# One meeting of the engines per stage boundary instead of two, with semaphore sets used in turn, in a two-block transformer kernel

## The reference

```
first block, for each of 2 layers:
    proj = rmsnorm(x) @ w_in
    y = sigmoid(gate_a) * (forgetting_attention(8 heads) @ w_o_fox)
      + sigmoid(gate_b) * (sparse_attention(8 heads, 2 kv heads) @ w_o_nsa)
    x = x + y @ w_out
    x = x + relu(rmsnorm(x) @ w_up) ** 2 @ w_down
x = rmsnorm(x)
second block, layer 0 (latent attention + gated linear attention), layer 1 (grouped-query attention):
    x = layer_norm(alpha * x + mix(x) @ w_o)
    ffn = 16 experts, each takes the 64 tokens with the highest affinity (SwiGLU, 1024 wide)
    ple = sigmoid(x @ ple_gate_w + b) * (p @ ple_w)
    x = layer_norm(alpha * x + ffn + ple)
```

## Time and profile before

| what | value |
| --- | --- |
| median of 3 runs | 3303.99 us (3303.64 to 3307.97) |
| profiled execution, its own time | 3308.26 us |
| span of the profile | 3306.4 us |
| PE busy | 3123.7 us (94%) |
| DVE, ACT, POOL busy | 1561.4, 1036.4, 238.5 us |
| mean granted TensorE clock | 0.979 |
| DMA | 590.24 MB, 47.3% of 16 engines' span |

### The profile page before, as it was taken

The page is one execution under the profiler, slowest core; times in us unless marked ns, Lnnn a source line. Parts: engine busy times, 40 slices in busy tenths (PEclk is TensorE's granted clock), DMA queues, the critical chain, the costliest instruction groups (busy, mean ns, idle before and its releaser), DMA issues. The chain is left out here.

```text
span 3306.4 us, 40198 instructions
## 1 busy us (share of the span) xinstructions
PE 3123.7 (94%) x15942; PEld 2132.1 (64%) x15942; DVE 1561.4 (47%) x2099; ACT 1036.4 (31%) x1645; POOL 238.5 (7%) x363
## 2 busy tenths in 40 slices
PE   6999999999999999999998999999989899999996
PEld 5886588888787568888785575444437457444442
DVE  3425558888522565888766461111126656111113
ACT  3325424445323624444443420010013543000002
POOL 1004300000101410000000200000000320000000
PEclk9999999999999999999998999999999999999999
DMA  6320123331440022333302147999992114799997
GB/s 160 117 64 27 64 83 108 103 103 63 133 136 30 1 94 85 102 102 102 117 8 67 51 160 301 421 422 422 422 386 65 58 64 173 324 421 422 422 422 312
DMA packets 234306, 590.24 MB, mean 179 GB/s; under 512 B 42966, under 2 KB 146332, under 8 KB 185004
## 3 DMA queue, kind: packets, MB, share of 16 engines
q1 hardware_dynamic: 234156, 588.16, 47.3%
HBM read 581.82 MB, written 2.10 MB: 177 GB/s over the span
## 5 line engine op out<-in xcount | busy, mean ns | idle before, releaser
L3016 PE MATMUL ps<-w_ring,xe 128*64 128x512 f32 x1024 | 234.0, 602 | 27.0 <-DMA w_ring<-in_w 21.9
L3016 PE MATMUL ps<-ex_front,xe 128*64 128x512 f32 x1024 | 232.9, 598 | 0.0
L3016 PE MATMUL ps<-ex_front,hidT 128*64 128x512 f32 x1024 | 225.6, 598 | 4.3 <-ACT hidT L3057 2.2
L1147 ACT ACTIVATE mlp_w_hi<-w_ring 128x2048 fp32r<-128x2048 f32 x86 | 165.4, 1927 | 187.2 <-PE ps L1084 71.5
L1249 DVE TENSOR_TENSOR mlp_w_lo<-w_ring,mlp_w_hi 128x2048 fp32r<-128x2048 f32 x86 | 196.6, 2288 | 43.8 <-ACT mlp_w_hi L1147 43.8
L350 PE MATMUL ps<-h_hi,in_w_hi 128*128 128x512 f32 (+1 forms) x528 | 207.0, 392 | 0.0
L350 PE MATMUL ps<-h_lo,in_w_hi 128*128 128x512 f32 (+1 forms) x528 | 205.6, 389 | 0.0
L350 PE MATMUL ps<-h_hi,in_w_lo 128*128 128x512 f32 (+1 forms) x528 | 205.6, 389 | 0.0
L1084 PE MATMUL ps<-h_hi,mlp_w_hi 128*128 128x512 f32 x512 | 199.7, 390 | 0.4 <-DVE h_lo L1355 0.4
L1084 PE MATMUL ps<-h_hi,mlp_w_lo 128*128 128x512 f32 x512 | 199.2, 389 | 0.0
L1084 PE MATMUL ps<-h_lo,mlp_w_hi 128*128 128x512 f32 x512 | 199.2, 389 | 0.0
(11 more groups left out here) (591 smaller groups left out, 6518.1 us busy)
## 6 DMA issues: line engine op xcount, KB each, us to landing
ex_front<-in_w SPq DMA_DIRECT2D x256, 1024.0 KB, 19.3
w_ring<-in_w SPq DMA_DIRECT2D x128, 1024.0 KB, 22.2
w_ring<-in_w_in SPq DMA_DIRECT2D x32, 1024.0 KB, 5.4
w_ring<-in_w_up SPq DMA_DIRECT2D x32, 1024.0 KB, 8.0
w_ring<-in_w_down SPq DMA_DIRECT2D x32, 1024.0 KB, 5.2
w_ring<-in_cmp_w SPq DMA_DIRECT2D x16, 512.0 KB, 4.8
w_ring<-in_w_out SPq DMA_DIRECT2D x8, 1024.0 KB, 6.0
w_ring<-in_w_o SPq DMA_DIRECT2D x8, 1024.0 KB, 9.5
```

The costliest lines, as they stand in the source:

```text
L1147: act.activation(w.hi[:, number(m, n) % HOMES, :], src, ACT.Copy).then_inc(s.hi_done, 1)
L3016: mm = pe.matmul(ps[rows, bank + half, :], lhsT, slot(2 * m + a)[:, kk, 512 * half:512 * half + 512], start=(k == 0), stop=(k == DC - 1))
```

## The change

`stage` no longer allocates semaphores and no longer clears them or meets at its end. Two banks of 48 semaphores are allocated once, in `build`, and stages take their names from the two banks in turn. A record of the semaphores of the stage just finished (`SEMS.used`, with the ring's used-up ready set) is kept. The next stage gets a SyncE body, ahead of its own SyncE program, that clears them, while the other engines are already at work in that stage with the other bank. The meeting at the end of the `Block` stays as it is. After the last stage `build` clears that stage's semaphores and lets the engines meet once more, as before.

```
-    with ExitStack() as ctx:
-        sems = {n: ctx.enter_context(nc.semaphore(f"{label}_{n}_{next(SERIAL)}")) for n in names.split()}
-        with nc.Block() as block:
-            yield block, Names(**sems)
-        for run in runs_of(list(sems.values()) + list(clear)):
-            nc.sync.sem_clear(run)
-        nc.all_engine_barrier(sem_only=True)
+    bank = SEMS.banks[SEMS.now]
+    SEMS["now"] ^= 1
+    sems = dict(zip(names.split(), bank, strict=False))
+    assert len(sems) == len(names.split())
+    with nc.Block() as block:
+
+        @block.sync
+        def _(sp):
+            for run in runs_of(SEMS.used):
+                sp.sem_clear(run)
+        yield block, Names(**sems)
+    SEMS["used"] = list(sems.values()) + list(clear)
...
+        SEMS.update(banks=[[ctx.enter_context(nc.semaphore(f"stage{a}_{n}")) for n in range(MOST_NAMES)] for a in range(2)], now=0, used=[])
         ps = ctx.enter_context(nc.psum_tensor("ps", [P, NB, BANK], F32))
         ring = Ring(nc, ctx)
...
+        for run in runs_of(SEMS.used):
+            nc.sync.sem_clear(run)
+        nc.all_engine_barrier(sem_only=True)
```

More of the change, by code:

```diff
@@ L108, in runs_of @@
     return runs
+SEMS = Names(banks=[], now=0, used=[])
+MOST_NAMES = 48
 @contextmanager
 def stage(nc, label, names, clear=()):
-    with ExitStack() as ctx:
-        sems = {n: ctx.enter_context(nc.semaphore(f"{label}_{n}_{next(SERIAL)}")) for n in names.split()}
-        with nc.Block() as block:
-            yield block, Names(**sems)
-        for run in runs_of(list(sems.values()) + list(clear)):
-            nc.sync.sem_clear(run)
-        nc.all_engine_barrier(sem_only=True)
+    bank = SEMS.banks[SEMS.now]
[9 more added lines that the diff above has]
+    SEMS["used"] = list(sems.values()) + list(clear)
 class Pair:
```

## The result

The changed kernel took 3282.59 us (median of 4 executions, 3280.07 to 3287.19), the kernel before 3305.98 beside it: ratio 0.9934, 95% interval 0.9918 to 0.995. With all executions on record together, 82 of the kernel before have a median of 3305.0 us (3295.8 to 3314.4) and 16 of the changed one 3287.1 (3280.1 to 3294.6): 17.8 us, 0.54%. The first four were lucky by some 4 us, and a single execution of either kernel says little: they spread by 15 to 19 us.

A forecast was written before the change was run, and what follows sets the result against it. The prediction took matrix work to bound the kernel (PE busy 3123.7 of 3306.4 us), untouched by the change. 9.8 us of stretches plus 0.3 of end clears gave 10.1 off the median 3303.99: 3293.9 us, range 3288 to 3300 (8 in 10).

The forecast's parts named there:

- The direct part: At the stage boundaries and program end: removed meetings and clears save 9.8 + 0.3 = 10.1 us.
- 22 stretches: Between the releases from first and second meeting at 22 of 23 boundaries: 0.37 to 0.64 us each, 9.8 us together.
- fewer clears at the end: At the end of the program: last clears go from eight to two or three, saving 0.3 us.
- the 355 ns: Skill's figure for a five-engine launch meeting, somewhat more than the rows leave (0.32 us); by it the sum would be 10.8 us.
- Its rule for the clears: At the second meetings: 0.37 us with one clear, 0.054 us for each further clear; 9.9 us over 22 stretches.
- The clock returns more: Rival at four TensorE waits: shorter idleness keeps the clock full, up to 6.8 us more, 3287.1 us; chance 0.12.
- the likeliest case: Whole kernel: a gain of 7 to 13 us, 3291 to 3297 us; chance 0.65.
- The price of a fall: Behind TensorE's waits at a boundary: each fall of the granted clock costs 1.7 us.
- The runs' own spread of 4 us: Whole kernel: three runs of one program lie up to 4.3 us apart; included in the partial gain's chance of 0.19.
- No part of the stretch came back: Rival at each boundary: part of the 0.37 us reappears elsewhere; if half, gain 5 us, 3298.9 us; chance 0.19.
- No first instruction came late: Rival at stage starts: second meeting hides instruction loading; exposed at all 22 boundaries it costs 22 us, 3315.9 us; chance 0.04.
- a transfer covered the boundary: At the two expert stages: a transfer already under way could cancel the gain, 1.3 us for both; loss put at nothing.

The follow-up runs named there:

- e1: Changed kernel with a second meeting after each of the 23 blocks again, without clears ahead of it: 3300.77 us, ratio 0.9985 to the kernel before.
- b1: The kernel before, unedited, run again for a second trace: 3297.82 us in 5 executions, ratio 0.9969 to the same kernel beside it.
- e3: The kernel before with only the two semaphore banks added; clears and second meeting stay at the end of the stage: 3300.75 us, ratio 0.9986.
- e5: Changed kernel with a second meeting, without clears, at nine of the 23 boundaries only: 3300.69 us, ratio 0.9981 to the kernel before.
- a1: The changed kernel, unedited, run again: 3288.61 us in 6 executions, ratio 0.995 to the kernel before.
- a2: The changed kernel, unedited, run again beside two other kernels: 3286.77 us in 6 executions, ratio 0.9944 to the kernel before.
- e8: Changed kernel with 30 identity transposes keeping TensorE busy at the end of both w_o stages: 3288.63 us, ratio 0.9951 to the kernel before.
- e9: Changed kernel with TensorE kept busy by transposes at the ends of both w_o, both pl, gs and the first expert stage: 3284.2 us, ratio 0.9938.

## Why the prediction was wrong

**The direct part was right.** Predicted: 9.8 us for 22 stretches and 0.3 for fewer clears at the end. At equal granted clock the executions can be compared without its falls: at 0.982, 14 of the kernel before have a median of 3297.8 us and 5 of the changed one 3287.2, 10.6 less; at 0.981 it is 9.6, at 0.980 10.8, from three and two executions of the changed kernel. The stages without a fall confirm it one by one: `ct` 2.90 to 2.53 and `n0` 8.55 to 8.14, 0.37 and 0.41. The clears at the end went from eight to three, and the last stretch from 0.76 to 0.47 us.

**One price in it was wrong without harm.** The prediction gave the first clear 0.054 us like every further one and was left with 0.32 us for a bare meeting. In e1 a bare meeting takes 0.37 us, so the rows leave room for the 355 ns that it had put aside as too much, and its sum of 10.8 us by that figure adds 22 first clears that cost nothing. The 9.8 us were read from the stretches themselves and do not hang on it. Its rule for the clears also adds up to 10.0 us, not 9.9.

**The clock's part was mis-sized, and this is the step that failed.** The sum had no term for the clock. The rival "The clock returns more" had the right mechanism and the chance 0.12, and named the wrong boundaries. It said that "the edge lies somewhere between 2.04 and 3.31" and looked for gains at the four waits of 3.3 to 3.5 us. Yet the earlier trace rows, which priced a fall, held falls near 818 and 2822 us, and the prediction did not read the wait ahead of these. It was 2.12 and 2.56 us. Its lower bound, the 2.04 us near 1871 with a whole clock behind them, was the luck of one trace: behind the same wait of 2.05 to 2.08 us the clock fell in b1, e1, e3 and e5. There is no sharp edge in these traces. Falls appear somewhere above 1.71 us, and the change carries five waits from 2.0 to 2.6 us down to 1.7 to 1.9. The long waits (now 2.94 to 3.07) still had falls behind them in 10 of 12 cases (after, a1, a2).

Luck made the miss larger and did not make it: the first four executions showed a gain of 23 us, all of them together 18, and both are above the 13 up to which the likeliest case went. The size of it: over all executions with a clock on record the mean clock is 0.9796 before and 0.9821 after. Over all kernels, the time falls by 2.7 us per 0.001 of clock at a given kernel. 2.5 × 2.7 = 6.8 us; with the 10.6 us of the direct part, 17.4 of the 17.8 us. That is an estimate, but the stages give the same in another way: the second `in` 1.2 us, `ei` 2.7 (two falls, the second one in its middle), the first expert stage 1.6 and the second `wy` 0 to 3, each beyond its meeting, 7.1 us over all stages.

**The price of a fall**, 1.7 us, nearly holds where TensorE is the bound: `wy` 89.8 to 91.4, `ei` 105.7 to 107.2 to 108.8. In the first `pl` it is 0.44 us, at the start of the first `w_o` nothing. Neither the prediction nor the expectations of e8 and e9 asked which engine bounds the work behind a fall. For the change it would have mattered little; in e8 and e9 it was a part of the error.

**The spread was mis-sized too.** "The runs' own spread of 4 us" came from three executions. It is 18.6 us over 82, and `gs` alone can make 7 of it.

**The other rivals.** No part of the stretch came back: the stages without a fall lost all of theirs. No first instruction came late: the first work of a stage starts at most 0.1 us after the release, as before. Whether a transfer covered the boundary ahead of the second expert stage can't be told, since that stage took 481.3 to 483.3 us in the three traces of the changed kernel. The Trainium skill (TensorE: Matmul & The Clock Gate, Part 1) has the clock fall after idleness, and how much then runs slow vary from run to run. The traces agree: the clock fell behind 18 of 25 waits of 2.04 to 2.57 us, not behind all, and not behind the same ones in two traces of one kernel.

**What stays open.** How much of the 7 us comes from each boundary, since a trace is one execution; why the second fall in `ei` goes with the first; whether the shorter wait ahead of `gs` makes its long form rarer; and why the first expert stage is longer by 1 us in e8 and e9.

## What to carry to other kernels

Ask of every idle stretch of TensorE, before and after a change, how long it is, and not only of those that the change seems made for: 0.4 us less at a wait of 2.1 us took away a fall worth some 1.2 us more. Compare kernels whose clock varies at equal granted clock, and with many executions: with four of each, 18 us looked like 23. A clock made whole behind a fall is worth something only if TensorE bounds the work there.

## What the runs showed of the hardware

The granted clock fell behind none of 21 waits of TensorE of 1.7 us, 4 of 12 of 1.92 us, 18 of 25 of 2.04 to 2.57 us and 5 of 5 of 2.8 to 3.0 us. The linear-attention stage took 49.6 to 49.9 us in some traces, with 11 to 14 us of them at 1.2 GHz, and 56.1 to 57.2 in others, with 27 to 28 us, in the kernel before and in the changed one alike. A meeting of five engines without clears and drain takes 0.37 us, and a single range clear inside it adds nothing; with six clears it takes 0.64. Two sets of executions of one identical kernel, taken side by side, had medians 12 us apart.
